# Packing the input gates, the forget gates and the low-rank gate input of a hybrid mLSTM/GLA layer into one 128-column weight tile

## What is computed

```python
def mlstm_prep(p, conv_w, b_gates, with_q):
    k = to_heads(jax.nn.silu(dw_conv(p[..., OFF_ML_K:OFF_ML_V], conv_w[:, ML_WIDTH:])), N_ML_HEADS)
    ...
    g = (p[..., OFF_ML_G:OFF_GLA_Q] + b_gates).astype(jnp.float32)
    g = g.reshape(bsz, t, 4, N_ML_HEADS).transpose(2, 0, 3, 1)
    fwd = (q, k, v, g[0], jax.nn.log_sigmoid(g[1]))
    bwd = (q, k, v, g[2], jax.nn.log_sigmoid(g[3]))

def gla_prep(p, w_a2, b_a, with_q):
    ...
    a_lr = p[..., OFF_GLA_A:PROJ_WIDTH]
    la_f = to_heads(jax.nn.log_sigmoid((a_lr[..., :GLA_RANK] @ w_a2[0] + b_a[0])...) / GLA_GATE_TAU, N_GLA_HEADS)
    la_b = to_heads(jax.nn.log_sigmoid((a_lr[..., GLA_RANK:] @ w_a2[1] + b_a[1])...) / GLA_GATE_TAU, N_GLA_HEADS)
```

## Time and profile before

| what | us |
|---|---|
| median of 3 runs | 1614.76 |
| lowest and highest of them | 1613.89 and 1615.92 |
| the profiled execution, its own time | 1622.58 |
| its span, first to last instruction | 1620.8 |

### The profile page before, as it was taken

The page is one execution under the profiler, slowest core; times in us unless marked ns, Lnnn a source line. Parts: engine busy times, 40 slices in busy tenths (PEclk is TensorE's granted clock), DMA queues, the critical chain, the costliest instruction groups (busy, mean ns, idle before and its releaser), DMA issues.

```text
span 1620.8 us, 22739 instructions
## 1 busy us (share of the span) xinstructions
PE 1353.2 (83%) x8526; PEld 1209.5 (75%) x8526; DVE 1048.6 (65%) x1313; ACT 767.2 (47%) x892; POOL 132.3 (8%) x127
## 2 busy tenths in 40 slices
PE   4896999898799996387599831999999999999980
PEld 1775889798689995276488720889988888998870
DVE  5638421299543541766631778788888888888865
ACT  5624220133211214456311430778778788878752
POOL 1000000110000001000040411001000010000003
PEclk9898999999899999599599975999999999999995
DMA  9100010000253430000320193899999999999965
GB/s 344 63 26 26 27 52 1 0 1 0 104 182 104 150 112 26 0 0 7 115 68 27 66 350 125 315 364 377 381 376 374 374 378 369 381 380 381 379 212 219
DMA packets 142117, 293.23 MB, mean 181 GB/s; under 512 B 4832, under 2 KB 94944, under 8 KB 139632
## 3 DMA queue, kind: packets, MB, share of 16 engines
q1 hardware_dynamic: 137456, 275.70, 47.0%
q0 software_dynamic: 4608, 16.78, 4.0%
HBM read 271.49 MB, written 20.97 MB: 180 GB/s over the span
## 4 chain that ended last, share of the span: by engine, by line
PE 74%; DVE 12%; issue 5%; ACT 4%; DMA 3%; POOL 1%; DVEq 0%; POOLq 0%; SPq 0%; ACTq 0%
PE psum L1876 21%; PE psum L1629 9%; PE psum L1670 5%; PE psum L1671 5%; PE psum L1672 5%; PE psum L1869 4%; PE psum L1867 4%; PE psum L1868 4%; DVE mask_add L1477 1%; DVE left L1480 1%; PE psum L1632 1%; PE psum L1772 1%; PE psum L1764 1%; PE psum L1701 1%; PE psum L1689 1%
## 5 line engine op out<-in xcount | busy, mean ns | idle before, releaser
L1497 DVE TENSOR_TENSOR e_lo<-e_raw,e_hi 128x2048 fp32r<-128x2048 f32 x192 | 434.1, 2288 | 45.9 <-ACT e_hi L985 44.8
L985 ACT ACTIVATE e_hi<-e_raw 128x2048 fp32r<-128x2048 f32 x192 | 362.9, 1913 | 70.6 <-PE psum L1876 51.6
L1670 PE MATMUL psum<-w_hi,h_hi 128*128 128x256 f32 x576 | 165.3, 287 | 0.5 <-issue 0.5
L1671 PE MATMUL psum<-w_hi,h_lo 128*128 128x256 f32 x576 | 164.7, 286 | 0.0
L1672 PE MATMUL psum<-w_lo,h_hi 128*128 128x256 f32 x576 | 164.6, 286 | 0.0
L1867 PE MATMUL psum<-e_hi,xt_hi 128*128 128x256 f32 x512 | 147.3, 288 | 0.0
L1869 PE MATMUL psum<-e_lo,xt_hi 128*128 128x256 f32 x512 | 144.8, 283 | 0.0
L1868 PE MATMUL psum<-e_hi,xt_lo 128*128 128x256 f32 x512 | 144.7, 283 | 0.0
L1670 PEld LDWEIGHTS psum<-w_hi,h_hi 128*128 128x128 f32 x576 | 112.3, 195 | 0.6 <-issue 0.6
L1671 PEld LDWEIGHTS psum<-w_hi,h_lo 128*128 128x128 f32 x576 | 112.3, 195 | 0.0
L1672 PEld LDWEIGHTS psum<-w_lo,h_hi 128*128 128x128 f32 x576 | 112.3, 195 | 0.0
(11 more groups left out here) (340 smaller groups left out, 2892.7 us busy)
## 6 DMA issues: line engine op xcount, KB each, us to landing
e_raw<-w_e_gate SPq DMA_DIRECT2D x64, 1024.0 KB, 15.4
e_raw<-w_e_up SPq DMA_DIRECT2D x64, 1024.0 KB, 12.8
e_raw<-w_e_down SPq DMA_DIRECT2D x64, 1024.0 KB, 13.2
ada_x<-w_ada SPq DMA_DIRECT2D x16, 1024.0 KB, 6.0
raw<-w_in_units SPq DMA_DIRECT2D x15, 1024.0 KB, 4.8
ada_raw<-w_ada SPq DMA_DIRECT2D x8, 1024.0 KB, 12.1
xs<-x SPq DMA_DIRECT2D x4, 1024.0 KB, 13.9
raw<-w_out_units SPq DMA_DIRECT2D x4, 1024.0 KB, 4.8
```

What stands on the lines that cost most here:

```text
L985: act.activation(e_hi[u % EH][:], e_raw[u][:], ACT.Copy).then_inc(e_hi_ok, 1)
L1497: dve.tensor_tensor(e_lo[u][:], e_raw[u][:], e_hi[u % EH][:], ALU.subtract).then_inc(e_lo_ok, 1)
L1670: pe.matmul(o, x_hi[:, k, c], w_hi[n % 2][:, k, :], start=k == 0, stop=False)
L1671: pe.matmul(o, x_lo[:, k, c], w_hi[n % 2][:, k, :], start=False, stop=False)
```

## The change

The 48 useful columns go into one tile of 128. Columns 0 to 3 and 32 to 35 hold the input gates of the two directions, 64 to 67 and 96 to 99 the forget gates, and 4 to 19 and 36 to 51 the low-rank columns of the two directions. Unit 8 is still loaded whole (1 MB), but its second half of columns is no longer used. Tile 0 is gone. What is left is computed as tile 1, in half 1 of PSUM, and raises `tile_mm` by 2 at its end, so all later tile numbers stay.

- TensorE: 72 matmuls less. The blocks of the transposes swap their halves, so that the gate tile still follows on a block in its own half. The waits for `h_ready` now stand in the gate tile.
- ScalarE waits for the one tile, writes `row_f` first (from partitions 64 to 127 of PSUM to partitions 0 to 63), then `gate_rows` from all 128. The three steps of the log-sigmoid and their counterpart on VectorE work on 64 partitions instead of 128; the number of elements in a row is the same.
- The host arranges the bias, `w_gla2` and the columns of unit 8 to match.

```diff
@@ scalar
             for k in range(KC):
                 act.wait_ge(xt_ready, k + 1)
-                s = k % 2
+                s = (k + 1) % 2
...
             split_hi(9)
-            for t in range(2):
-                act.wait_ge(tile_mm, t + 1)
-                dst = gate_rows if t == 0 else row_f
-                act.activation(dst[:, 0:CTX], t_ctx(t), ACT.Identity, bias=col("b_gates")[:, t:t + 1])
-                act.activation(dst[:, CTX:ALL], t_lat(t), ACT.Identity, bias=col("b_gates")[:, t:t + 1]).then_inc(g_free, 1)
+            act.wait_ge(tile_mm, 2)
+            for dst, q in ((row_f[0:64, :], slice(64, P)), (gate_rows[:], slice(0, P))):
+                act.activation(dst[:, 0:CTX], t_ctx(1)[q, :], ACT.Identity, bias=col("b_gates")[q, 0:1])
+                act.activation(dst[:, CTX:ALL], t_lat(1)[q, :], ACT.Identity, bias=col("b_gates")[q, 0:1]).then_inc(g_free, 1)
             split_hi(10)
             act.wait_ge(g_free, 2)
 
-            act_link(act.activation(row_a[:], row_f[:], ACT.Abs))
-            act_link(act.activation(row_a[:], row_a[:], ACT.Exp, scale=-1.0))
-            act.activation(row_a[:], row_a[:], ACT.Ln, bias=1.0).then_inc(row_act, 1)
+            act_link(act.activation(row_a[0:64, :], row_f[0:64, :], ACT.Abs))
+            act_link(act.activation(row_a[0:64, :], row_a[0:64, :], ACT.Exp, scale=-1.0))
+            act.activation(row_a[0:64, :], row_a[0:64, :], ACT.Ln, bias=1.0).then_inc(row_act, 1)
@@ vector
-            link(dve.scalar_tensor_tensor(row_f[:], row_f[:], 0.0, row_a[:], ALU.min, ALU.subtract))
+            link(dve.scalar_tensor_tensor(row_f[0:64, :], row_f[0:64, :], 0.0, row_a[0:64, :], ALU.min, ALU.subtract))
@@ tensor
             def x_block(k):
 
-                s = k % 2
+                s = (k + 1) % 2
...
                 for k in range(KC):
-                    if i == 0:
+                    if n == 8:
                         pe.wait_ge(h_ready, k + 1)
...
-            t_unit(8, 0, True, None)
+            unit_ready(8)
+            t_tile(1, 8, 0, True).then_inc(tile_mm, 2)
             t_unit(9, 2, True, g_free)
@@ host
+        g[:, 32 * d + NH:32 * d + NH + RANK] = w[:, OFF_A + RANK * d:OFF_A + RANK * (d + 1)]
```

More of the change, by code:

```diff
@@ L724, in _ @@
                 act.wait_ge(xt_ready, k + 1)
-                s = k % 2
+                s = (k + 1) % 2
                 if k >= 2:
                     act.wait_ge(h_ready, k - 1)
-                act.activation(h32[:, s, 0:CTX], t_ctx(s), ACT.Identity, bias=modc[:, k, 1:2],
+                act.activation(h32[:, k % 2, 0:CTX], t_ctx(s), ACT.Identity, bias=modc[:, k, 1:2],
                                scale=amix[:, 1, k:k + 1])
-                act.activation(h32[:, s, CTX:ALL], t_lat(s), ACT.Identity, bias=modc[:, k, 0:1],
+                act.activation(h32[:, k % 2, CTX:ALL], t_lat(s), ACT.Identity, bias=modc[:, k, 0:1],
                                scale=amix[:, 0, k:k + 1]).then_inc(h32_ready, 1)
@@ L1925, in small_array @@
     for kind in range(2):
-        bg[0:NH, kind], bg[32:32 + NH, kind] = g[kind], g[2 + kind]
+        for d in range(2):
+            bg[64 * kind + 32 * d:64 * kind + 32 * d + NH, 0] = g[2 * d + kind]
     w2 = np.zeros((P, 2 * GK_W), np.float32)
     for d in range(2):
-        w2[64 + RANK * d:64 + RANK * (d + 1), GK_W * d:GK_W * (d + 1)] = a["w_gla_a2"][0, d]
+        w2[32 * d + NH:32 * d + NH + RANK, GK_W * d:GK_W * (d + 1)] = a["w_gla_a2"][0, d]
     parts = {
@@ L1949, in unit_arrays @@
             o = OFF_G + NH * (2 * d + kind)
-            g[:, P * kind + 32 * d:P * kind + 32 * d + NH] = w[:, o:o + NH]
-    g[:, 64:64 + 2 * RANK] = w[:, OFF_A:OFF_A + 2 * RANK]
+            g[:, 64 * kind + 32 * d:64 * kind + 32 * d + NH] = w[:, o:o + NH]
+        g[:, 32 * d + NH:32 * d + NH + RANK] = w[:, OFF_A + RANK * d:OFF_A + RANK * (d + 1)]
     starts = [OFF_K, OFF_K + UW, OFF_Q, OFF_Q + UW, OFF_V, OFF_V + UW, OFF_GK, OFF_GQ, OFF_GV, OFF_GV + UW,
```

## The result

The changed kernel took 1604.56 us (median of 5 runs, 1600.27 to 1607.71) against 1615.92 us for the kernel before (5 runs, 1613.89 to 1619.3): a ratio of 0.9919, with a 95% interval from 0.9894 to 0.9945. In microseconds that is 11.4 less by the medians, and between 8.9 and 17.1 less by the interval. Timed a second time, against 17 runs of the kernel before, the same kernel had a ratio of 0.9912 (0.9892 to 0.9933), 14.3 us between the medians (1605.22 and 1619.54). The forecast was 14.1 us less, at 1600.7 us in a range from 1598.0 to 1604.0. The median lies 0.6 us above that range; the ratio, taken on the 1614.76 us from which the forecast started, gives 1601.7 us and lies inside it. What follows separates the size of the change, which was right, from the scatter, which was not.

The account below looks back on a forecast made before the run. TensorE bounds up to the last gate tile's end, then the row chain to tile 4. Tile −14.08, emptying, new wait and partitions 0 each: −14.08 us off the 1614.76 median gives 1600.7 us, range 1598 to 1604.

Parts of the forecast that it names:

- The chain: Gate tile's end to tile 4: unit 10's transfer and rounding, row chain, VectorE's taps; 42.05 us against TensorE's 28.1 us.
- T: The end of the last gate tile, where unit 10's transfer starts; forecast to move from 117.16 to 103.08.
- The tile: The gate tile that goes, a full tile at full clock ahead of T: −14.08 us.
- The emptying: ScalarE empties PSUM twice after T, inside its wait for unit 10, with 1.6 us to spare: 0 us.
- the half partitions: Abs, Exp, Ln and VectorE's first instruction on 64 partitions: no gain, since row length sets the time.
- the new wait: TensorE stops about 1.6 us ahead of tile 2 for the gate tile's emptying, hidden under the row chain: 0 us.
- The new stop: TensorE's stop ahead of tile 2, from T to about T + 1.6, forecast to cost nothing.
- The margin: TensorE's idle time ahead of tile 4, forecast to shrink from 13.9 to 12.3 us and still hold.
- The clock: Tile 2 may drop to 1.2 GHz, 2.7 us within the idle time; tile 4's slow head may vary by 0.6 us.
- TensorE as the bound at tile 4: Rival: clock stays at 1.2 GHz through tiles 2 and 3; gain only 3.6 us, 1611.2 us; chance 0.03.
- the slower case: Rival: clock stays low from the stop ahead of tile 2 through tiles 2 to 5; 17 us slower, about 1632; chance 0.02.
- swallowed further down: Rival: a later stage, perhaps the experts' loads, turns the 14 us into waiting; 1614.8 us; chance 0.04.

Follow-up runs that it names:

- the pair of kernels with the tile ahead of and behind T: The change with 72 matmuls put back: gate tile computed twice, 1620.06 us (0.9995 to before); or tile 2 computed twice, 1603.76 us (0.9905).
- The early taps: The change with the first two key tiles' taps moved into the row chain, instead of behind it: 1591.89 us, 0.9848 to the kernel before.
- before, taps early: The kernel before, both gate tiles kept, with the first two key tiles' taps moved into the row chain: 1602.09 us, 0.9911.
- taps early, tile 2 twice: The change with taps moved into the row chain and tile 2 computed twice: 1604.87 us, 0.9911 to the kernel before.

## Why the prediction was right

**The chain.** It was read rightly: T to tile 4 is 42.03 us against 42.05, with the same links. The instants that were forecast (gate tile's end near 103.1, row chain's head near 116.1, tile 4 at about 145.1) all came 2.9 us earlier, by the head start of the gate tile. The pair of kernels with the tile ahead of and behind T shows, rather than argues, that the gain comes from T and not from TensorE's load.

**The tile.** Forecast −14.08 us; measured −14.05 between the gate tile's start and T.

**The emptying, the half partitions, the new wait.** Forecast at zero each. The emptying left 1.74 us of the wait for unit 10 (1.6 forecast). The forecast added up the lengths of the two pieces, 0.47 and 1.11, to 1.58 us; by the rows the second starts before the first has ended, and the pair takes 1.49 (117.16 to 118.65). Two such pairs taken off the 4.74 us of the transfer leave 1.76 us. Half the partitions changed nothing: the log-sigmoid's steps take 1.26, 1.27 and 1.27 us on 64 partitions and 1.25, 1.27 and 1.27 on 128, VectorE's first instruction 1.49 us on either, and the shift between partitions costs nothing either. The new stop was 1.65 us (1.6 forecast), and taking it away brought tile 4 no nearer to T as long as the row chain was the later path. The early taps show the other half of that sentence: with the cover gone it costs 1.87 us.

**The margin.** 12.3 us forecast; 12.04 us measured.

**The clock.** The fear that the new stop would lower the clock in tile 2 was not borne out: 1.00 throughout tiles 2 and 3. The slow head of tile 4 was still there and went away only when the stop was filled or removed. Heads of bursts did differ from trace to trace where the instructions up to there were the same: the gate tile took 17.0 us in most traces, and 15.7 in the one without tile 2's wait, whose gate tile is unchanged, with a mean clock of 0.91 against 0.83:

```profile
82.60:98.30 15.70, 15.70 (x74) 13.27 (x75) 9.36 (x8) 3.50 (x4) 0.00 (x0) 0.91 0.00 1
```

With the tile twice ahead of T the first of the two took about 15.8 (29.92 less 14.1). Tile 4's head scattered too: from its start to the statistics it was 73.76 us before, 73.99 in the change, and 73.12 and 73.14 in these two traces. So a head moves by 1.3 us without an edit to it, twice the 0.6 us that the prediction allowed; what decides it was not looked for. That the heads before and after were nearly alike (17.0 and 17.0, 73.76 and 73.99) is luck that the forecast had. The rule of the Trainium skill that it cited (TensorE: Matmul & The Clock Gate, Part 1: The HAM clock gate: the number of slow matmuls at a burst's head differs between runs of one kernel) agrees with these traces, as far as kernels that are the same up to that head can stand for one kernel.

**The term that was mis-sized** is the run's scatter. The prediction took it from three runs of the kernel before, 0.9 us below to 1.2 us above the median, and subtracted from their median. The 17 runs of the second timing lie between 1615.27 and 1625.7, and their median is 4.8 us above the 1614.76 of the three. Whether these came from the same chip as the three is not on record, so the 4.8 us may hold a difference between chips besides scatter. Either way 1600.7 us was a forecast against a low sample, while the difference of 14.1 us holds: it lies inside both intervals, and the second comparison gives 14.3. The range, 1598 to 1604, was too narrow for the same reason: the median of the change fell 0.6 us outside it, and only the ratio puts it inside. The profiled start of the gate tile moves between 82.35 and 86.11 us over the ten traces, and what follows the statistics takes between 1383.7 us (before, taps early: 1596.8 − 213.12) and 1388.7 us (taps early, tile 2 twice: 1606.1 − 217.39) without an edit there. Where in those stretches the scatter arises was not followed up.

**The rivals.** TensorE as the bound at tile 4 did not happen, nor did the slower case: the clock held. The gain was not swallowed further down: the last stretch of both traces is alike, and since that stretch scatters by 5 us, the better evidence is the pair with and without the tile ahead of T, 14.8 us apart by their medians (1605.22 and 1620.06).

## What to carry to other kernels

A tile that is removed is worth its time only on the path that ends last: find the instant from which two paths leave, and ask on which side of it the tile stands. To test such a reading, put the same work back once on each side; a total that cares about the place settles it where the shares of busy time can't. And when a path is found to be covered by a longer one, look next at why the longer one is that long: here the taps for which tile 4 waited stood behind 35 row instructions whose results TensorE did not need before the statistics, and moving the taps won as much again as the change.

## What was not expected of the hardware

Three runs of a kernel agreed within 2 us and were still 5 us from the median of seventeen taken later, perhaps on another chip. The clock's slow stretch at the head of a burst is another source of scatter, 1.3 us at the gate tile and 0.8 us at tile 4 in these traces. For differences under one per cent, compare marks inside the traces besides the medians: the two profiles of the change agree within 0.03 us between the gate tile's start and the statistics (133.02 and 133.05), while its own runs spread over 7 us.
